# A two-layer encoder trunk: first attention with interleaved score products, norm factors spread by transposes, first two projection blocks begun chunk by chunk

## The reference

```
x = x + 0.5 * swiglu_ffn(rms_norm(x, ffn1_norm[l]), ...)
h = rms_norm(x, mix_norm[l])
y = swa_sink_attention(h, ...) if l == 0 else mla_attention(h, ...)
x = x + y
x = x + 0.5 * swiglu_ffn(rms_norm(x, ffn2_norm[l]), ...)
```

```
q = apply_rope(q, cos, sin); k = apply_rope(k, cos, sin)    # [x1*c - x2*s, x2*c + x1*s]
logits = q . k * 64**-0.5       # 64 queries x 128 keys per chunk and head
probs = softmax([logits, sink])[..., :-1];  out = probs . v;  y = out @ w_out
```

## Time and profile before

| what | us |
|---|---|
| median of three runs (1840.41 to 1841.6) | 1840.58 |
| the profiled execution | 1839.91 |
| its span, first to last instruction | 1838.1 |
| TensorE busy in the span | 1808.4 (98%) |
| VectorE busy | 914.1 (50%) |
| ScalarE busy | 623.0 (34%) |
| GpSimd busy | 148.8 (8%) |
| stretch 0 to 20.98: TensorE busy | 8.60 |
| stretch 395 to 510: TensorE busy | 108.79 |

### The profile page before, as it was taken

How to read it: one execution, slowest core, us unless ns; L and a number is a source line. 1 busy time by engine, 2 the same in 40 slices (tenths; PEclk the granted TensorE clock), 3 DMA queues, 4 the chain that set the end, 5 groups by cost and what they waited for, 6 DMA issues and landing times.

```text
span 1838.1 us, 23399 instructions
## 1 busy us (share of the span) xinstructions
PE 1808.4 (98%) x8601; PEld 1479.7 (80%) x8601; DVE 914.1 (50%) x1407; ACT 623.0 (34%) x1044; POOL 148.8 (8%) x124
## 2 busy tenths in 40 slices
PE   7999999999999999999999999999999999999998
PEld 5888888877788888888888888888766788888886
DVE  5443433468654434335543343456897544344344
ACT  5422222335543223223322222233466442222222
POOL 0100100012101001000110010100000010010010
PEclk9999999999999999999999999999999999999999
DMA  6333333233233333332333333234111333333321
GB/s 173 109 95 99 92 103 89 83 106 84 76 97 95 100 92 102 97 92 86 103 103 94 98 94 103 83 94 113 30 40 58 92 102 101 95 91 103 92 83 55
DMA packets 322097, 169.94 MB, mean 92 GB/s; under 512 B 13362, under 2 KB 317679, under 8 KB 322031
## 3 DMA queue, kind: packets, MB, share of 16 engines
q1 hardware_dynamic: 321680, 168.26, 32.0%
q10 hardware_dynamic: 350, 0.83, 0.1%
HBM read 162.50 MB, written 2.10 MB: 90 GB/s over the span
## 4 chain that ended last, share of the span: by engine, by line
PE 64%; issue 29%; DVE 3%; DMA 2%; POOL 1%; SPq 1%; ACT 0%; POOLq 0%; DVEq 0%; ACTq 0%
PE bank L1077 21%; PE bank L1078 21%; PE bank L1079 21%; POOL work L458 1%; DVE work L934 1%; DMA w_raw<-b_kvup 1%; SPq L388 0%; DMA r_kv<-work 0%; DMA work<-x 0%; PE bank L1195 0%; PE bank L1105 0%; DVE w_lo L710 0%; PE bank L1182 0%; PE bank L1094 0%; DMA m_q<-work 0%
## 5 line engine op out<-in xcount | busy, mean ns | idle before, releaser
L1077 PE MATMUL bank<-h_hi,w_hi 128*128 128x512 f32 x1536 | 601.2, 391 | 1.9 <-issue 1.7
L1079 PE MATMUL bank<-h_hi,w_lo 128*128 128x512 f32 x1536 | 598.3, 390 | 0.0
L1078 PE MATMUL bank<-h_lo,w_hi 128*128 128x512 f32 x1536 | 598.2, 389 | 0.0
L710 DVE TENSOR_TENSOR w_lo<-w_raw,w_hi 128x1024 fp32r<-128x1024 f32 (+2 forms) x320 | 394.4, 1233 | 317.1 <-ACT w_hi L518 309.0
L518 ACT ACTIVATE w_hi<-w_raw 128x1024 fp32r<-128x1024 f32 (+2 forms) x320 | 319.5, 998 | 296.1 <-PE bank L1079 296.0
L1077 PEld LDWEIGHTS bank<-h_hi,w_hi 128*128 128x128 f32 x1536 | 288.8, 188 | 62.3 <-issue 2.2
L1079 PEld LDWEIGHTS bank<-h_hi,w_lo 128*128 128x128 f32 x1536 | 288.6, 188 | 60.3
L1078 PEld LDWEIGHTS bank<-h_lo,w_hi 128*128 128x128 f32 x1536 | 288.9, 188 | 59.1
L1077 PE MATMUL bank<-y_hi,w_hi 128*128 128x512 f32 x832 | 325.1, 391 | 0.9 <-DVE xT L782 0.7
L1079 PE MATMUL bank<-y_hi,w_lo 128*128 128x512 f32 x832 | 323.8, 389 | 0.0
L1078 PE MATMUL bank<-y_lo,w_hi 128*128 128x512 f32 x832 | 323.7, 389 | 0.0
(11 more groups left out here) (136 smaller groups left out, 972.7 us busy)
## 6 DMA issues: line engine op xcount, KB each, us to landing
w_raw<-ffn_gu SPq DMA_DIRECT2D x176, 512.0 KB, 3.8
w_raw<-ffn_d SPq DMA_DIRECT2D x64, 512.0 KB, 3.7
w_raw<-ffn_d SPq DMA_DIRECT2D x32, 384.0 KB, 3.3
w_raw<-a_in SPq DMA_DIRECT2D x10, 512.0 KB, 3.9
w_raw<-a_out SPq DMA_DIRECT2D x8, 512.0 KB, 3.7
w_raw<-b_out SPq DMA_DIRECT2D x8, 512.0 KB, 3.6
w_raw<-b_in SPq DMA_DIRECT2D x5, 512.0 KB, 3.9
w_raw<-b_qup SPq DMA_DIRECT2D x16, 144.0 KB, 2.3
```

What stands on the lines that cost most here:

```text
L710: last = v.tensor_tensor(w_lo[:, sl, 0:k, 0:m], w_raw[:, sl, 0:k, 0:m], w_hi[:, sl, 0:k, 0:m].bitcast(F32), ALU.subtract)
L1077: t.matmul(b[:, :], wh, hi[:, c, :], start=c == 0, stop=False)
L1078: t.matmul(b[:, :], wh, lo[:, c, :], start=False, stop=False)
L1079: last = t.matmul(b[:, :], wl, hi[:, c, :], start=False, stop=c == k - 1)
```

## The change

1. Start: SP loads x chunk pair 0, weight block 0, x 1, weight block 1, x 2 and 3. TensorE transposes chunks 0 to 5 into six banks (`XB`), then runs for chunk c the high-weight products of blocks 0 and 1 and transposes chunk c + 6; the products with the low weights follow for both blocks. ScalarE makes `h_hi` of every chunk and `xT` of the even ones, VectorE `xT` of the odd ones. Squares all lie on ScalarE, their adds after the low parts of blocks 0 to 2. The sums come after six chunks of block 2, the spread after five chunks of block 3. ScalarE makes high(3) and VectorE low(3) ahead of the feed-forward's loop.
2. Norm factors: `spread` transposes the factor column, repeated over 128 columns, with the identity; the diagonals are gone. It waits for the last factor step.
3. First attention: the cosine and sine tables are multiplied by `r_x` once on VectorE; ScalarE copies the raw block (`raw`), for pair p + 1 between its two copies of transposes. For c >= 2 the exchange is issued half by SP (now before the weight load of that turn) and half by ScalarE, and VectorE adds (`rotated`), where GpSimd did. Score products alternate between the two heads (partitions 0 to 63 and 64 to 127, banks 3 and 4) within each chunk; transposes have banks of their own (5 and 6), and scores of pair p wait for the exponentials of pair p - 1. VectorE's low part of weights stands after the normalisations.

```diff
@@ TensorE, scores of the first attention
-                for e in range(2):
-                    if p > 0:
-                        pe.wait_ge(pt_done, 2 * (p - 1) + e + 1)
-                    rows = slice(e * HD, (e + 1) * HD)
-                    for c in range(NC):
+                if p > 0:
+                    pe.wait_ge(exp_done, 2 * p)
+                for c in range(NC):
+                    for e in range(2):
+                        rows = slice(e * HD, (e + 1) * HD)
                         o = c % 2 * CHUNK
                         last = t.matmul(SC[e][o:o + CHUNK, c // 2 * P:(c // 2 + 1) * P],
                                         qt_a[rows, (1 + p) % 2, c * CHUNK:(c + 1) * CHUNK],
                                         kpad[rows, p // 4, c * CHUNK:c * CHUNK + P], start=True, stop=True)
-                    last.then_inc(s_full, 1)
+                        if c == NC - 1:
+                            last.then_inc(s_full, 1)
@@ TensorE, transposes of the probabilities
-                        last = t.transpose(SC[e][:, i * P:(i + 1) * P], p_a[e][:, i * P:(i + 1) * P], ident)
+                        last = t.transpose(TA[e][:, i * P:(i + 1) * P], p_a[e][:, i * P:(i + 1) * P], ident)
@@ TensorE, spread
-                pe.wait_ge(diag_ready, count["stat"])
+                pe.wait_ge(nstep, 4 * count["stat"])
-                    last = t.matmul(MISC[:, i * P:(i + 1) * P], ones[:, :], diag[:, i, :], start=True, stop=True)
+                    last = t.transpose(MISC[:, i * P:(i + 1) * P], st[:, 5, i:i + 1].to_broadcast([P, P]), ident)
@@ TensorE, first feed-forward
-                            normed(n, 0)
-                            normed(n, 1, lambda: sums(m, KD), 3)
-                            spread(m + 1)
-                            normed(n, 2)
-                            normed(n, 3)
+                            normed(n, 2, lambda: sums(m, KD), 6)
+                            normed(n, 3, lambda: spread(m + 1))
@@ TensorE, start
+            for k in range(6):
+                x_transposed(k)
+            for c in range(KD):
+                pe.wait_ge(h_ready, c + 1)
+                for n in range(2):
+                    if c == 0:
+                        pe.wait_ge(hi_done, n + 1)
+                    b, wh = bank[RING[n][0]][:, :], w_hi[:, n, c, :]
+                    t.matmul(b, wh, h_hi[:, c, :], start=c == 0, stop=False)
+                    t.matmul(b, wh, h_lo[:, c, :], start=False, stop=False)
+                if c + 6 < KD:
+                    x_transposed(c + 6)
+            for n in range(2):
+                pe.wait_ge(split_done, n + SLOTS + 1)
+                for c in range(KD):
+                    last = t.matmul(bank[RING[n][0]][:, :], w_lo[:, n, c, :], h_hi[:, c, :],
+                                    start=False, stop=c == KD - 1)
@@ the exchange, called by SP for parts 0 and 1 and by ScalarE for 2 and 3 (c >= 2)
+        def exchange(eng, n, c, parts):
+            eng.wait_ge(evac_done, block_a(n, c) + FIRST + 1)
+            if c >= 2:
+                eng.wait_ge(rot_done, c - 1)
+            for x in parts:
+                y = x ^ 1
+                eng.dma_start(swapped[c % 2][x * ROPE_B:(x + 1) * ROPE_B, :],
+                              raw_a[y * ROPE_B:(y + 1) * ROPE_B, c % 2, :]).then_inc(swap_in[c % 2], 16)
@@ ScalarE, per pair
                         act.wait_ge(t_full, 2 * (p - 1) + e + 1)
-                        a.activation(pt_a[:, e, :], SC[e][:, :], ACT.Copy).then_inc(pt_done, 1)
+                        a.activation(pt_a[:, e, :], TA[e][:, :], ACT.Copy).then_inc(pt_done, 1)
+                        if e == 0 and p + 1 < PAIRS:
+                            raw(2 + p)
                 if p + 1 < PAIRS:
+                    exchange(act, n, 2 + p, (2, 3))
                     high(n + 3 + p + AHEAD)
@@ VectorE, rotary
+            def rotated(c):
+                dve.wait_ge(sine_done, c + 1)
+                dve.wait_ge(t1_done, c + 1)
+                q = qt_a[:, c % 2, :]
+                v.tensor_tensor(q, q, swapped[c % 2][:, :], ALU.add).then_inc(rot_done, 1)
+            v.tensor_tensor(cos_a, cos_a, r_x[:, :], ALU.mult).then_inc(table_r, 1)
+            v.tensor_tensor(sin_a, sin_a, r_x[:, :], ALU.mult).then_inc(table_r, 1)
```

More of the change, by code:

```diff
@@ L40 @@
 AHEAD = 3
-FIRST = TT * 2
+FIRST = 0
 C_ID, C_CA = 0, P
@@ L381, in swap @@
             def swap(c):
[L383 to L389, removed]
+                exchange(sp, k_block, c, range(4) if c < 2 else (0, 1))
             for j in range(2, 2 + PAIRS + KD):
+                if 9 <= j < 8 + PAIRS:
+                    swap(j - 7)
                 if j < 2 + PAIRS:
@@ L521, in high @@
                 last.then_inc(hi_done, 1)
-            count = {"sq": 0, "add": ADDS_START, "tiles": 0}
+            count = {"sq": 0, "add": 0, "tiles": 0}
             def squared(src, first):
@@ L563, in up @@
                                          ACT.Copy).then_inc(hid_hi, 1)
-                    repeat(act, tiles // 2, up, last=True)
+                    repeat(act, tiles // 2, up, first=n == 0, last=True)
                     count["tiles"] += tiles
@@ L594, in _, with raw @@
             act.wait_ge(t_in, 32)
-            for k in range(3):
-                high(n + k + AHEAD)
+            def raw(c):
+                blk = block_a(n, c)
+                act.wait_ge(pe_done, blk + FIRST + 1)
+                if c >= 2:
+                    act.wait_ge(rot_done, c - 1)
+                a.activation(raw_a[:, c % 2, :], bank[RING[blk][0]][:, :], ACT.Copy).then_inc(evac_done, 1)
+            high(n + AHEAD)
+            raw(0)
+            high(n + 1 + AHEAD)
+            act.wait_ge(evac_done, n + 1 + FIRST + 1)
+            high(n + 2 + AHEAD)
+            raw(1)
             for p in range(PAIRS + 1):
@@ L762, in rms_values @@
                 refine()
-                if spread:
-                    for i in range(TT):
-                        last = v.tensor_scalar(diag[:, i, :], ident, st[:, 5, i:i + 1], None, ALU.mult)
-                    last.then_inc(diag_ready, 1)
                 count["stat"] += 1
@@ L862, in _ @@
[L862 to L869 removed]
+            for k in range(KD):
+                src = xT[:, k, :]
+                if k % 2 == 0:
+                    dve.wait_ge(x_even, k // 2 + 1)
+                else:
+                    dve.wait_ge(x_hi, k + 1)
+                    src = XB[k % 6][:, :]
+                    v.tensor_copy(xT[:, k, :], src)
+                v.scalar_tensor_tensor(h_lo[:, k, :], src, gT[:, G_FFN1 + k:G_FFN1 + k + 1],
+                                       h_hi[:, k, :].bitcast(F32), ALU.mult, ALU.subtract).then_inc(h_ready, 1)
@@ L870, in _ @@
+            for n in range(AHEAD):
+                low(n)
+            for k in range(KD):
+                added(k == 0)
+            low(AHEAD)
             dve.wait_ge(ready0, 4)
             n = ffn(0, 0, G_MIX)
-            def scaled_a(c):
-                b = product(block_a(n, c))
-                if c >= 2:
-                    dve.wait_ge(rot_done, c - 1)
-                v.tensor_tensor(raw_a[:, c % 2, :], b[:, :], r_x[:, :], ALU.mult).then_inc(evac_done, 1)
             def sine_a(c):
+                dve.wait_ge(table_r, 2)
```

131 lines of the change are left out of this document (65 added, 66 removed).

## The result

| | before | after |
|---|---|---|
| median (lowest to highest, 4 runs each) | 1840.49 us (1839.73 to 1841.6) | 1828.23 us (1827.58 to 1828.58) |
| span of the profiled execution | 1838.1 us | 1825.8 us |
| after / before | | 0.9933 (0.9915 to 0.9950) |

12.3 us less, where 14.5 were forecast. Behind the first attention 10.15 of the 10.7 us forecast up to there had come. The rest fell short at the other norms, where 2.2 us were lost in one place that no term of the sum had: the norm of the second attention's query latents.

The account below looks back on a forecast made before the run. TensorE was taken as the bound (busy 1808.4 of 1838.1 us), with VectorE nearly full in the attention. Gains of 1.8 + 8.9 + 3.8 = 14.5 us gave 1825.4, or 1826.1 against the median; range 1820 to 1833 (8 in 10).

Parts of the forecast that it names:

- Start: First projection: first product 5 us earlier, at 16.0, but a 2.7 us wait before block 4; gain 1.8 us.
- First attention: Shorter score groups (1.0 us for 1.78) and a shorter VectorE chain, periods 8.7 for 9.42: 8.9 us in all.
- S0 to S7: First attention, from the start of the first scores to that of the last: 59.6 us forecast for 67.65.
- The 0.3 after S7: After the last scores start, TensorE waits for the second normalisation, leaving 0.3 us of the 0.78 saved there.
- Late chain: First attention: exchange lands at 3.9 us each time, six pairs wait 0.85 us, 1831.3 us; chance 0.10.
- Serial scores: First attention: score products still stream one after another, only waits go, 3.8 instead of 8.9 us, 1831.2; chance 0.16.
- Four-fold scores: First attention: all four quarters stream side by side, 0.45 to 0.5 us a score group, 1823 us; chance 0.08.
- Stuck issues: First attention: ScalarE held at its two DMA issues, period 11.2 us, about 1845 us in all; chance 0.06.
- Six other norms: Norms outside start and first attention: 6 x 0.40 for spreads plus 1.4 for diagonal waits, 3.8 us (1.4 to 5.0).

Follow-up runs that it names:

- x_early: Changed kernel with block 4's weights split before the first norm factors (high part on ScalarE, low part on VectorE): 1826.42 us, ratio 0.9919 to the kernel before.
- x_heads: Changed kernel with the score products of a pair head by head again, banks and waits as changed: 1832.57 us, ratio 0.9954 to the kernel before.
- x_rows: Changed kernel with score products alternating only the row half; the column half changes once, after eight products: 1832.48 us, ratio 0.9953 to the kernel before.
- x_cross: Changed kernel with score products alternating head 0 even chunk and head 1 odd for eight products, then the other diagonal: 1831.82 us, ratio 0.9945.
- x_quad: Changed kernel with score products ordered head 0 even chunk, head 0 odd, head 1 even, head 1 odd: 1828.31 us, ratio 0.9928 to the kernel before.
- x_kpe: Changed kernel with the second attention's third and fourth key/value weight blocks issued ahead of the four rotary key broadcasts: 1825.01 us, ratio 0.9915.
- x_later: Changed kernel with the sums of the query latents' norm one value half later, transfer untouched: 1828.41 us, ratio 0.9927 to the kernel before.
- x_sp: Changed kernel with all four transfers of each exchange issued by SP again: 1829.94 us, ratio 0.9943 to the kernel before.
- x_diag: Changed kernel with the diagonals and four fp32 products back in all eight spreads of norm factors: 1833.06 us, ratio 0.9955 to the kernel before.
- x_pool: Changed kernel with the rotary addition on GpSimd again for every pair: 1830.27 us, ratio 0.9937 to the kernel before.

## Why the prediction came out as it did

- **Start (forecast 1.8 us, 1.65 measured).** Right in each of its steps, the price (the wait for block 4's low half) too. x_early shows that this price was avoidable.
- **First attention (forecast 8.9, 8.6 measured, from a lead of 1.52 at its own sums to 10.15).** S0 to S7 59.57 for 59.6, period 8.67 for 8.7, group 1.03 for 1.0. That S0 to S7 fits so closely is two errors that cancel: one late landing made a period 9.05, and the last period took 7.81 for the 8.15 forecast. The size was right, a reason for it was wrong, and that 1.0 was met is therefore luck: I read 55.6 ns a record as serial streaming and let the alternation of row halves pay by itself. x_heads shows that 0.26 of the 1.78 us was a hidden wait, x_rows that rows alone give nothing, x_cross and x_quad that four different quarters in a row are what pays. The 0.3 after S7 did not come (10.18 and 10.15 us of lead).
- **Late chain (rival, 0.10).** Its mechanism exists, but in one pair of seven. The chain that ended last in that pair, kernel after (start, us, what):

```profile
442.69 3.92 DMA m_q<-work
...
446.71 0.70 DVE m_q L901
...
449.19 0.66 PE bank L1232 x4
```

A landing of 3.92 us made that period 9.05 instead of 8.67; in x_quad the same landing took 4.44 and the period 9.59, 0.5 of the 1.4 us by which its span is longer. In x_kpe no period was so. It is not the bound of the stage.
- **Serial scores (rival, 0.16).** Fell by the group of 1.03 us. Its price would have been near right: x_heads and x_rows lie at 1832.5 for its 1831.2.
- **Four-fold scores (rival, 0.08).** Fell too: 1.03 us, where it asked for 0.45 to 0.5.
- **Stuck issues (rival, the slower side).** No issue of the exchange on ScalarE stood long: the longest took 0.87 us where the forecast had 0.59, and two together 1.42, below the 2.3 from which the rival lets TensorE wait.
- **Six other norms (forecast 3.8, 2.2 measured, the step that failed).** Behind the first attention the lead grew from 10.15 to 12.36. Of the terms, 6 x 0.44 for the spreads and 1.4 for the two waits of the diagonals can be read off: 4.0. But the longer of those waits, 0.85, came back as 0.84 at the query latents, and 1.36 us of matmuls at 1.2 GHz with it, 2.2 together; 0.4 of gain came in small steps that I assign to nothing. The term was sized by the instructions removed; it lacked what is late next once those waits are gone, a transfer queued behind four broadcasts. The row to look at stood in the trace before (1288.66, quoted above): the sums already waited 0.30 for VectorE, so any lead that the transfer did not share had no slack left. x_kpe removed the transfer's delay and with it the loss.

What stays open is why matmuls run at 1.2 GHz behind some waits and not behind others. At the query latents (x_later: one block on) a slow stretch stood behind seven of ten waits of 0.80 to 1.91 us and in none of the three traces that wait 0.30 or not at all; behind the wait of block 4 (2.63 to 2.69 us) it stood in three of ten. After the same 2.68 us wait of block 4 they stayed fast in the kernel after, and did not in x_heads, timeline of TensorE:

```profile
44.08 0.49 PE L1102 MATMUL bank<-h_hi,w_hi 128*128 128x512 f32 x1 [2.68 <-DVE w_lo L743]
45.34 0.63 PE L1104 MATMUL bank<-h_hi,w_lo 128*128 128x512 f32 x1
45.76 0.63 PE L1102 MATMUL bank<-h_hi,w_hi 128*128 128x512 f32 x1
```

The two kernels have the same instructions up to there. The Trainium skill ("TensorE: Matmul & The Clock Gate", Part 1: The HAM clock gate) ties the clock to how busy the engine has been; the slow stretches named here all stand behind an idle one, which agrees, but nothing in these runs tells beforehand which wait draws one.

## What to carry to other kernels

When a change brings the bounding engine somewhere earlier, list the places further on where it already waits a few tenths, and follow each back to its transfer: there part of the gain can be given back, and moving one transfer ahead of a bulk of others can be worth more than the instructions saved (3.2 us here for a reordering of six issues). Products on 64x64 quarters should go round all four quarters (1.03 us a group); two in turn, whichever two, took 1.52. A group's time divided by its records is not the rate of the engine as long as a wait may stand inside the group; separate the banks first, then read it.

## What the runs showed of the hardware

- 32 fp32 records of 64x64 with 128 moving columns: 1.52 us on two quarters in turn (by column, row or diagonal), 1.03 us in both orders that visit four.
- After waits of 1.1 to 2.7 us inside a kernel that is 99% busy, matmuls ran at half speed (0.63 us each, 0.43 apart) for about 3 to over 6 us, after some of these waits and not after others (none after 1.71 us in x_sp). With it, waits of 1.14 and 1.91 us cost 2.8 and 5.1 (the stretch measured against x_kpe's 7.95), that of 2.68 about 4.3.
- A transpose of a repeated column moves 128 columns of factors for half of a product with a diagonal: 0.36 us for four against 0.80, and takes no work of VectorE.
- Pieces of 64 KB landed in 2.0 and 2.3 us at the median (issued by SP and by ScalarE), but those of one exchange in 3.9 to 4.5 us at the same place in six kernels, and of single other ones in three kernels (x_diag, x_pool, x_later). A late landing costs only what the matmuls beside it don't cover.
